# Four adaLN norms of a two-layer trunk: the x times root product moves from GpSimd to VectorE, ScalarE writes the high half, and each third of the tokens is refined just ahead of its own tiles

## The reference

```python
def rms_norm(x, g):
    xf = x.astype(jnp.float32)
    y = xf * lax.rsqrt(jnp.mean(xf * xf, axis=-1, keepdims=True) + EPS)
    return (y * g.astype(jnp.float32)).astype(x.dtype)

def trunk_layer(x, mod, g1, g2, ...):
    shift1, scale1, gate1, shift2, scale2, gate2 = jnp.split(mod, 6, axis=-1)
    h = rms_norm(x, g1) * (1 + scale1) + shift1
    mix, new_ctx = token_mixers(h, w_in, ...)      # starts with h @ w_in
    x = x + gate1 * mix
    h = rms_norm(x, g2) * (1 + scale2) + shift2
    x = x + gate2 * ((silu(h @ w_gate) * (h @ w_up)) @ w_down)
```

## Time and profile before

| | |
|---|---|
| three runs, median | 3786.46 us (3783.27 to 3788.51) |
| profiled execution, its own time | 3774.25 us |
| its span | 3772.4 us |
| PE busy | 3450.7 us (91%) |
| DVE busy | 1783.7 us (47%) |
| POOL busy | 892.0 us (24%) |
| ACT busy | 747.6 us (20%) |
| mean granted TensorE clock | 0.949 |

### The profile page before, as it was taken

How to read it: one execution, slowest core, us unless ns; L and a number is a source line. 1 busy time by engine, 2 the same in 40 slices (tenths; PEclk the granted TensorE clock), 3 DMA queues, 4 the chain that set the end, 5 groups by cost and what they waited for, 6 DMA issues and landing times.

```text
span 3772.4 us, 49780 instructions
## 1 busy us (share of the span) xinstructions
PE 3450.7 (91%) x17864; PEld 2974.1 (79%) x17864; DVE 1783.7 (47%) x2702; ACT 747.6 (20%) x1334; POOL 892.0 (24%) x526
## 2 busy tenths in 40 slices
PE   6798599998969999999969977999987999999998
PEld 3787455556969999999968864555586999999998
DVE  1744566665164333433364356666534434333433
ACT  2322233333130000000042132333312000000001
POOL 1411111112242222222142101111123322222220
PEclk9898799998989999999989897999988999999999
DMA  5243724333101111111013354334120111111111
GB/s 182 70 138 105 219 83 122 87 106 87 42 28 39 44 44 42 36 44 44 23 41 122 119 183 131 90 113 117 52 84 28 45 44 44 44 35 42 44 33 50
DMA packets 304119, 287.72 MB, mean 76 GB/s; under 512 B 65650, under 2 KB 250820, under 8 KB 303988
## 3 DMA queue, kind: packets, MB, share of 16 engines
q1 hardware_dynamic: 274036, 248.94, 22.8%
q10 hardware_dynamic: 29952, 37.17, 2.7%
HBM read 236.39 MB, written 49.79 MB: 76 GB/s over the span
## 4 chain that ended last, share of the span: by engine, by line
PE 83%; DVE 8%; issue 4%; DMA 2%; ACT 1%; SPq 1%; ACTq 0%; DVEq 0%
PE ps L1626 21%; PE ps L1628 21%; PE ps L1627 21%; PE ps L1861 8%; PE ps L1881 4%; DVE neg_max L1474 4%; PE ps L1667 1%; DVE h_hi L1278 1%; PE ps L1688 1%; PE ps L1901 1%; PE ps L1846 1%; PE ps L1845 1%; PE ps L1652 1%; PE ps L1890 1%; DVE h_lo L1280 0%
## 5 line engine op out<-in xcount | busy, mean ns | idle before, releaser
L1626 PE MATMUL ps<-h_hi,w_hi 128*128 128x384 f32 (+1 forms) x3072 | 1065.1, 347 | 118.3 <-DVE h_lo L1280 104.5
L1627 PE MATMUL ps<-h_lo,w_hi 128*128 128x384 f32 (+1 forms) x3072 | 1043.6, 340 | 0.0
L1628 PE MATMUL ps<-h_hi,w_lo 128*128 128x384 f32 (+1 forms) x3072 | 1042.7, 339 | 0.0
L1626 PEld LDWEIGHTS ps<-h_hi,w_hi 128*128 128x128 f32 (+1 forms) x3072 | 583.1, 190 | 135.4 <-issue 116.5
L1627 PEld LDWEIGHTS ps<-h_lo,w_hi 128*128 128x128 f32 (+1 forms) x3072 | 582.9, 190 | 11.6 <-issue 1.3
L1628 PEld LDWEIGHTS ps<-h_hi,w_lo 128*128 128x128 f32 (+1 forms) x3072 | 582.2, 190 | 3.2
L1566 DVE SCALAR_TENSOR_TENSOR x<-ps,lmod,x 128x384 f32<-128x384 f32 (+2 forms) x768 | 365.9, 511 | 318.1 <-PE ps L1628 318.0
L1590 DVE TENSOR_TENSOR wk<-ps,wk 128x384 f32<-128x384 f32 x132 | 73.6, 558 | 839.6 <-PE ps L1628 835.1
L924 POOL CAST w_hi<-w_stage 128x1024 fp32r<-128x1024 f32 x120 | 124.9, 1041 | 1060.2 <-PE ps L1628 701.4
L1132 ACT ACTIVATE p_t<-ps 128x512 f32<-128x512 f32 (+1 forms) x456 | 264.7, 580 | 504.7 <-PE ps L1628 265.5
L1626 PE MATMUL ps<-act_hi,w_hi 128*128 128x384 f32 x1056 | 356.9, 338 | 0.0
(11 more groups left out here) (247 smaller groups left out, 4280.8 us busy)
## 6 DMA issues: line engine op xcount, KB each, us to landing
ada_buf<-in_w_ada SPq DMA_DIRECT2D x96, 512.0 KB, 6.2
w_stage<-in_w_ffn_gate SPq DMA_DIRECT2D x44, 512.0 KB, 3.8
w_stage<-in_w_ffn_up SPq DMA_DIRECT2D x44, 512.0 KB, 3.8
w_stage<-in_w_ffn_down SPq DMA_DIRECT2D x44, 512.0 KB, 3.7
s_in<-ev_p ACTq DMA_DIRECT2D x66, 192.0 KB, 2.6
w_stage<-in_w_in SPq DMA_DIRECT2D x24, 512.0 KB, 4.0
ada_w<-in_w_ada SPq DMA_DIRECT2D x4, 2048.0 KB, 17.0
w_stage<-in_w_out SPq DMA_DIRECT2D x16, 512.0 KB, 4.9
```

Of the source, the lines that this page charges most:

```text
L1626: nc.tensor.matmul(out, wh, xh, start=first, stop=False)
L1627: nc.tensor.matmul(out, wh, xl, start=False, stop=False)
L1628: return nc.tensor.matmul(out, wl, xh, start=False, stop=last)
```

## The change

- The product of x, gain gs and root rs is one DVE instruction (mul), or two in the first third. norm_mul is gone; in its place POOL waits for the end of the norm, so that no weight unit is split beside it.
- ACT adds the shift alone and writes the result straight to h_hi, rounded. The DVE copy L1278 is gone.
- DVE computes h_lo as (wk + shift) - h_hi in one instruction (low), again two in the first third.
- DVE's order is mul(i + 1), low(i). newton of a third stands in mul of its first tile, so between low(6) and mul(8), and so on. root of the next third stands in ACT's program behind the third's fifth tile.

```diff
-                def norm_mul(n0, stat0):
-                    pool.wait_ge(sq_used, n0 + G * DK + 4)
-                    for i in range(G * DK):
-                        ...
-                        pool.tensor_tensor(wk[:, i % 4, :], x[:, k, cols(g)], rs[:, g, :], ALU.mult)\
-                            .then_inc(nx_mul, 1)
...
-                norm_mul(l * (2 * G * DK), l * STATS)
+                pool.wait_ge(nx_done, l * (2 * G * DK) + G * DK)
...
-                norm_mul(l * (2 * G * DK) + G * DK, l * STATS + STATS - G)
+                pool.wait_ge(nx_done, (l + 1) * (2 * G * DK))
...
-                for g in range(G):
+                def root_x(g):
                     act.wait_ge(sq_used, n0 + 4 + (G * DK - G + g + 1 if which == 1 else (g + 1) * DK))
                     root(stat0 + g, 5 + g, D_MODEL)
+                root_x(0)
                 for i in range(G * DK):
                     g, k = divmod(i, DK)
                     act.wait_ge(nx_mul, n0 + i + 1)
                     for c, c0, c1 in halves(g):
-                        v = wk[:, i % 4, c0 - g * GW:c1 - g * GW]
-                        ins = nc.scalar.activation(v, v, ACT.Identity, bias=lmod[:, 24 * which + k, c:c + 1],
-                                                   scale=gs[:, which, k, c:c + 1])
-                    ins.then_inc(nx_mod, 1)
+                        ins = nc.scalar.activation(h_hi[:, k, c0:c1], wk[:, i % 4, c0 - g * GW:c1 - g * GW],
+                                                   ACT.Identity, bias=lmod[:, 24 * which + k, c:c + 1])
+                    ins.then_inc(nx_hi, 1)
+                    if k == DK - 4 and g + 1 < G:
+                        root_x(g + 1)
...
-            def split_norm(n0):
-                for i in range(G * DK):
-                    g, k = divmod(i, DK)
-                    dve.wait_ge(nx_mod, n0 + i + 1)
-                    nc.vector.tensor_copy(h_hi[:, k, cols(g)], wk[:, i % 4, :]).then_inc(nx_hi, 1)
-                    dve.wait_ge(nx_hi, n0 + i + 1)
-                    nc.vector.tensor_tensor(h_lo[:, k, cols(g)], wk[:, i % 4, :], h_hi[:, k, cols(g)].bitcast(F32),
-                                            ALU.subtract).then_inc(nx_done, 1)
+            def norm_split(stat0, n0, which):
+                def mul(i):
+                    g, k = divmod(i, DK)
+                    if k == 0:
+                        newton(stat0 + g, g)
+                        dve.wait_ge(stat_rs, stat0 + g + 1)
+                    for c, c0, c1 in halves(g):
+                        ins = nc.vector.scalar_tensor_tensor(
+                            out=wk[:, i % 4, c0 - g * GW:c1 - g * GW], in0=x[:, k, c0:c1],
+                            scalar=gs[:, which, k, c:c + 1], in1=rs[:, g, c0 - g * GW:c1 - g * GW],
+                            op0=ALU.mult, op1=ALU.mult)
+                    ins.then_inc(nx_mul, 1)
+                def low(i):
+                    g, k = divmod(i, DK)
+                    dve.wait_ge(nx_hi, n0 + i + 1)
+                    for c, c0, c1 in halves(g):
+                        ins = nc.vector.scalar_tensor_tensor(
+                            out=h_lo[:, k, c0:c1], in0=wk[:, i % 4, c0 - g * GW:c1 - g * GW],
+                            scalar=lmod[:, 24 * which + k, c:c + 1], in1=h_hi[:, k, c0:c1].bitcast(F32),
+                            op0=ALU.add, op1=ALU.subtract)
+                    ins.then_inc(nx_done, 1)
+                dve.wait_ge(sq_used, n0 + G * DK + 4)
+                mul(0)
+                for i in range(G * DK):
+                    if i + 1 < G * DK:
+                        mul(i + 1)
+                    low(i)
...
-                for g in range(G):
-                    newton(l * STATS + g, g)
-                split_norm(l * (2 * G * DK))
+                norm_split(l * STATS, l * (2 * G * DK), 0)
...
-                for g in range(G):
-                    newton(l * STATS + STATS - G + g, g)
-                split_norm(l * (2 * G * DK) + G * DK)
+                norm_split(l * STATS + STATS - G, l * (2 * G * DK) + G * DK, 1)
```

More of the change, by code:

```diff
@@ L380, in build @@
         newt_a, newt_b, stat_rs = sem("newt_a"), sem("newt_b"), sem("stat_rs")
-        nx_mul, nx_mod, nx_hi, nx_done = sem("nx_mul"), sem("nx_mod"), sem("nx_hi"), sem("nx_done")
+        nx_mul, nx_hi, nx_done = sem("nx_mul"), sem("nx_hi"), sem("nx_done")
         u_loaded, u_split = sem("u_loaded"), sem("u_split")
```

## The result

| | before | after |
|---|---|---|
| runs, median | 3784.86 us (4 runs, 3774.67 to 3788.51) | 3725.3 us (4 runs, 3724.59 to 3731.33) |
| profiled execution, its own time | 3774.25 | 3724.59 |
| its span | 3772.4 | 3722.8 |
| mean granted clock | 0.949 | 0.952 |

The ratio is 0.9848, with a 95% interval of 0.9828 to 0.9868. The forecast was 3738, and 3728 to 3757 its range: faster by more, and just outside.

A forecast was written before the change was run, and what follows sets the result against it. PE was taken as the bound, so the change acts only on its waits, mostly for DVE's h_lo. 2 x (7.5 + 16.3) = 47.6, say 48 us, off the runs' 3786.5 gave 3738; range 3728 to 3757.

The forecast's parts named there:

- The sum: Savings of both norms over two layers: 2 x (7.5 + 16.3) = 47.6, say 48 us; held for 67 in 100.
- t0: The end of a norm's first refinement: 91.83 us in norm 1 and 1043.48 in norm 2 before the change.
- norm 2, saved a layer: Third third starts 14.6 us earlier, plus 2.0 for the half-clock start, less 0.3: 16.3 us a layer.
- second start at half clock: Norm 2's third third: PE's slow start after 7.55 us idle goes, 15 matmuls taking 2.6 instead of 4.60: 2.0 us.
- PE goes on at job 0: Norm 1, tile 6: PE waits for job 0's squares, whose loads follow POOL's splits; on at t0 + 47.1, before 54.7.
- norm 1, saved a layer: Input projection: PE goes on at job 0 at t0 + 47.1 instead of t0 + 54.7, 7.5 us a layer.
- two thin margins of norm 2: Second and last thirds are ready 0.6 and 1.0 us before PE is through with the third ahead of each.
- the 0.3 taken off for them: Deduction of 0.3 us from norm 2's saving because its margins of 0.6 and 1.0 us are thin, leaving 16.3.
- the handshakes: Rival, 12 in 100: each low starts only once the instruction ahead has ended, 1.24 us a tile; saves 29, 3757.
- the half rate: Rival: DVE's scalar-tensor-tensor with two non-bf16 SBUF sources runs at half throughput; 26 us lost, 3812.
- the queue: Rival, 10 in 100: splits or loads behind them take 7 us more, norm 1 saves nothing; 33 us remain, 3753.
- More than the sum: Rival, 6 in 100: PE waits nowhere behind its first start and the clock is up sooner; 55 us, 3731.

The follow-up runs named there:

- the repeat at 3783.27: The kernel before, unchanged, run and profiled once more: profiled execution 3783.27 us; median of its 12 runs 3775.24, ratio 0.9993.
- the 82 runs: All runs of the unchanged kernel before, made beside every group of experiments: median 3777.9 us, 28 of them above 3781.
- two edits: Changed kernel with second third's refinement behind the first third (alone 3728.85 us) and weight units 4 and 5 split ahead of norm 1's end (alone 3720.74): both 3718.34.

## Why the prediction was wrong where it was, and right elsewhere

**The step that failed** is the last one of the sum: "The runs' median is 12 higher, and the verdict is on runs: 3786.5 - 48 = 3738". The three runs lay 9 to 14 us above the profiled execution, and I took that for a part of the kernel that the change would keep. By their times they were on the upper level, a layer at 1138 matmuls in 200 us. They have no profile of their own, but the repeat at 3783.27 has one and shows it; the profiled execution didn't have it, nor, by their times, did three of the changed kernel's four runs. From the profiled execution the same sum gives 3726; measured are 3725.3 (median) and 3724.59 (its own time). The text had both numbers and a difference of 12 us that it did not explain, and its range allowed 5 us for the spread of the runs, where the 82 runs spread over 22. That all three first runs were upper ones, where 28 of 82 are, was bad luck; to build on them beside a profile that said otherwise was the mistake.

**The sum** held: 49.6 us between the two spans, forecast 47.6. Point by point:

| | forecast | measured |
|---|---|---|
| DVE instruction, 384 columns; tile; tile in the first third | 0.61; 1.06; 1.32 | 0.62; 1.06; 1.32 |
| PE's first start, t0 + | 14.0 | 13.4 |
| third third starts, t0 + | 33.5 | 32.5 |
| norm done, t0 + | 32.5 | 31.7 |
| norm 2, saved a layer | 16.3 | 17.8 and 17.1 |
| second start at half clock | 2.0 | 2.2 and 1.4 |
| PE goes on at job 0, t0 + | 47.1 | 48.2 and 47.7 |
| norm 1, saved a layer | 7.5 | 8.8 and 8.2 |

- PE's start: ACT's pair took 0.80 and not 0.98, and the root between tiles cost nothing, so the whole schedule is 0.6 to 0.8 early. The two thin margins of norm 2 held, with no wait at the second or third third, and the 0.3 taken off for them was not lost.
- Saved a layer: from t0 of norm 2 to the next layer's first sum 868.75 became 850.96, and from t0 to the end of the span 887.50 became 870.41. The half-clock term: from its first matmul to the next third's, the third third takes 8.3 us in the changed kernel, where it took 10.5 and 9.7.
- Norm 1: POOL and SP did what was forecast, POOL's splits from 125.62 in 3.47 each, L588 at t0 + 39.8:

```profile
125.62 1.04 POOL L845 CAST w_hi<-w_stage 128x1024 fp32r<-128x1024 f32 x1 [52.88 <-DVE h_lo L1282]
129.09 1.04 POOL L845 CAST w_hi<-w_stage 128x1024 fp32r<-128x1024 f32 x1
```

```profile
133.45 0.69 SPq L588 DMA_DIRECT2D win_tab<-in_t_rope_gqa  x1
```

  From there PE took 8.4 us, not 7.36, and it had come 1.1 us sooner than forecast, so it waited 2.7 us where under 1 was forecast. By the moment at which PE goes on, norm 1 saved 6.4 and 7.2 us, less than the 7.5. The stretch from t0 of norm 1 to t0 of norm 2 shortened by 8.8 and 8.2 all the same, but with the same code it took 942.9 in one profile and 946.0 in another, so these two are no better than 3 us, and that they come out above 7.5 is not explained.
- The saved 51.9 is 49.6 in the spans mostly because the first norm's sums took 17.4 us and not 15.8 ahead of t0, the same code at a granted clock of 0.75 from 73 to 78 us, where the kernel before had 1.00.
- The rivals: the handshakes didn't show (DVE was never idle for more than 0.15 us within a norm's steady part), the half rate neither, and the queue let PE go on 1.1 and 0.6 us later than forecast, not 7. *More than the sum*, at 6 in 100, named 3731 for a reason that isn't the one seen.

## What to carry to other kernels

When the profiled execution and the other runs of a kernel differ by more than the measurement's own uncertainty, take the sum from the profiled one and ask what the difference is before carrying it over: counting matmuls in equal stretches of two profiles of one kernel, one on each level, would have shown it here. An engine's relief is worth what the next one in turn lets through: taking GpSimd out of a two-engine turn, with the new order, gave 18 us, and taking the cast off the engine that was left gave 32; of these 50, refinement per third is 8, and alone it gives nothing that can be measured. An earlier start counts only where the queues behind it are moved too (some 7 us for two edits of which one alone gave 4.4 and the other nothing).

## What the runs showed of the hardware

- Back-to-back matmuls of 384 columns at clock 1.00, PE busy without a gap, run at 1152 or at 1138 in 200 us with the down matmuls between them, which don't differ themselves. A start behind a wait, at either clock, can change it (173.3 to 176.7 ns a matmul), and it stays as long as PE goes on with them. What decides which of the two comes is open.
- DVE and POOL still take turns in the FFN, where POOL's splits now fall together with DVE's halves just behind norm 2. DVE's timeline:

```profile
1074.10 1.97 DVE L1601 CAST act_hi<-wk 128x384 fp32r<-128x384 f32 x1
1076.10 1.27 DVE L1603 TENSOR_TENSOR act_lo<-wk,act_hi 128x384 fp32r<-128x384 f32 x1
```

  The subtraction takes 0.56 and the cast 0.36 where POOL is idle. The Trainium skill (SBUF — State Buffer, Who interferes with whom) says that a DVE instruction with two SBUF inputs contends with a GpSimd one that reads SBUF. The trace agrees, with 1.24 to 1.27 for 0.56.
